# Five sets of seven products and one plain stretch in a SwiGLU layer, with three weight sums formed in device memory

## The reference

```python
x = x + merged @ w_o[layer]
h = rms_norm(x, ffn_norm_g[layer])
x = x + (jax.nn.silu(h @ w_ffn_gate[layer]) * (h @ w_ffn_up[layer])) @ w_ffn_down[layer]
return rms_norm(x, final_norm_g)
```

## Time and profile before

| | us |
|---|---|
| median of three runs | 377.54 (377.19 to 377.69) |
| the profiled execution | 377.2 |
| its span on the core | 375.4 |
| PE busy | 367.1 (98%) |
| DVE busy | 321.5 (86%) |
| ACT busy | 230.7 (61%) |
| POOL busy | 41.4 (11%) |
| data moved | 74.80 MB |
| granted TensorE clock | 0.995 of full speed |

### The profile page before, as it was taken

One profiled execution on the slowest core, in us unless ns is written; L12 is line 12 of the kernel. 1 busy time (PEld: TensorE's weight loads), 2 busy tenths in 40 slices (PEclk: granted clock), 3 DMA queues, 4 the chain that ended last, 5 costly groups with the idle time before them and its releaser, 6 DMA issues.

```text
span 375.4 us, 4744 instructions
## 1 busy us (share of the span) xinstructions
PE 367.1 (98%) x1847; PEld 309.0 (82%) x1847; DVE 321.5 (86%) x372; ACT 230.7 (61%) x267; POOL 41.4 (11%) x41
## 2 busy tenths in 40 slices
PE   7999999999999999999999999999999999999993
PEld 6998888788888888888888888888888888888882
DVE  4989987989867999989769669999999999999525
ACT  5767787676265956645447436955782892878205
POOL 2798020000000104000100000100100100000002
PEclk9999999999999999999999999999999999999998
DMA  8997255945270493899717902794796599360002
GB/s 284 282 296 266 60 182 207 320 143 210 57 281 0 66 345 120 321 353 308 281 55 276 358 39 55 179 384 172 184 359 236 129 308 347 113 248 33 0 2 112
DMA packets 41293, 74.80 MB, mean 199 GB/s; under 512 B 2316, under 2 KB 14648, under 8 KB 41272
## 3 DMA queue, kind: packets, MB, share of 16 engines
q1 hardware_dynamic: 38944, 70.03, 53.2%
q0 software_dynamic: 2112, 4.19, 6.6%
q10 hardware_dynamic: 216, 0.28, 0.2%
HBM read 73.46 MB, written 1.05 MB: 198 GB/s over the span
## 4 chain that ended last, share of the span: by engine, by line
PE 95%; DMA 1%; DVE 1%; issue 1%; POOL 0%; ACT 0%; POOLq 0%; SPq 0%; DVEq 0%; ACTq 0%
PE pp L1685 12%; PE pp L1687 12%; PE pp L1686 12%; PE pa L2069 7%; PE pa L2067 7%; PE pa L2068 7%; PE pp L1676 4%; PE pp L1665 3%; PE pp L1678 2%; PE pa L1676 2%; PE pa L2012 2%; PE pa L2010 2%; PE pa L1685 2%; PE pa L1687 2%; PE pa L2011 2%; PE pa L1686 2%
## 5 line engine op out<-in xcount | busy, mean ns | idle before, releaser
L1088 DVE TENSOR_TENSOR w_lo<-w_raw,w_hi 128x2048 fp32r<-128x2048 f32 x33 | 75.3, 2293 | 10.2 <-ACT w_hi L697 10.1
L970 ACT ACTIVATE w_hi<-w_raw 128x2048 fp32r<-128x2048 f32 x33 | 62.7, 1908 | 24.3 <-DVE w_raw L1536 24.3
L1556 DVE TENSOR_TENSOR w_lo<-w_raw,w_hi 128x2048 fp32r<-128x2048 f32 x33 | 74.6, 2283 | 0.2 <-ACT w_hi L970 0.2
L697 ACT ACTIVATE w_hi<-w_raw 128x2048 fp32r<-128x2048 f32 x33 | 62.6, 1912 | 19.6 <-DMA w_raw<-in_w_in 9.2
L1685 PE MATMUL pp<-w_hi,yT_hi 128*128 128x512 f32 (+1 forms) x104 | 40.5, 390 | 0.0
L1687 PE MATMUL pp<-w_lo,yT_hi 128*128 128x512 f32 (+1 forms) x104 | 40.3, 388 | 0.0
L1686 PE MATMUL pp<-w_hi,yT_lo 128*128 128x512 f32 (+1 forms) x104 | 40.3, 387 | 0.0
L1685 PE MATMUL pp<-w_hi,hT 128*128 128x512 f32 x96 | 38.0, 396 | 0.0
L1687 PE MATMUL pp<-w_lo,hT 128*128 128x512 f32 x96 | 37.4, 390 | 0.0
L1686 PE MATMUL pp<-w_hi,hT 128*128 128x512 f32 x96 | 37.4, 389 | 0.0
L2067 PE MATMUL pa<-w_hi,hT 128*128 128x512 f32 x64 | 24.9, 389 | 0.0
(11 more groups left out here) (341 smaller groups left out, 780.5 us busy)
## 6 DMA issues: line engine op xcount, KB each, us to landing
w_raw<-in_w_in SPq DMA_DIRECT2D x20, 1024.0 KB, 5.4
w_raw<-in_w_ffn_gate SPq DMA_DIRECT2D x11, 1024.0 KB, 8.9
w_raw<-in_w_ffn_up SPq DMA_DIRECT2D x11, 1024.0 KB, 8.5
w_raw<-in_w_ffn_down SPq DMA_DIRECT2D x11, 1024.0 KB, 7.9
w_raw<-in_w_o SPq DMA_DIRECT2D x4, 1024.0 KB, 5.3
x_sb<-in_w_ffn_gate POOLq DMA_DIRECT2D x3, 1024.0 KB, 9.3
w_raw<-in_w_out_attn SPq DMA_DIRECT2D x2, 1024.0 KB, 9.8
w_raw<-in_w_out_mlstm SPq DMA_DIRECT2D x2, 1024.0 KB, 5.2
```

The lines of the kernel that those rows point to most:

```text
L697: nc.scalar.activation(w_hi[:, slot_of(c), :], early_raw(c), ACT.Copy).then_inc(hi_ready, 1)
L970: nc.scalar.activation(w_hi[:, slot_of(c), :], form_raw(name, p), ACT.Copy).then_inc(hi_ready, 1)
L1088: nc.vector.tensor_tensor(w_lo[:, slot_of(c), :], early_raw(c), w_hi[:, slot_of(c), :].bitcast(F32), ALU.subtract).then_inc(lo_ready, 1)
L1556: nc.vector.tensor_tensor(w_lo[:, slot_of(c), :], form_raw(*FORM[c]), w_hi[:, slot_of(c), :].bitcast(F32), ALU.subtract).then_inc(lo_ready, 1)
```

## The change

Of the three plain stretches one stays and a fifth set takes the place of the two others: 256 plain columns and 2560 in sets. The first set now begins right behind the one plain stretch. Its sums `T1`, `T3` (here as `B22 + B12`) and `T2` are no longer made by DVE. Each is formed in a tensor `formed` in device memory, early in the kernel: SP copies one block there (`form_copy`), and POOL adds the other by an adding transfer (`form_grow`), written with the four rows of blocks `k` as the outermost index; the sums are then loaded like any chunk, `T2` straight into `x_sb`. POOL issues two of these adding transfers ahead of that of the mLSTM gate and the third right behind it. The splits run four chunks ahead of PE in place of five, and three during the first set. Some semaphores are merged to stay within their number, so that DVE's first use of the gate columns also waits for the biases.

```diff
-SETS = 4
-PLAIN = 3
+SETS = 5
+PLAIN = 1
+AHEAD_FORMED = {("T1", 0): ("B12", "B11"), ("T3", 0): ("B22", "B12"), ("T2", 0): ("B22", ("T1", 0))}
+STORED = {form: n for n, form in enumerate(AHEAD_FORMED)}
...
-    names = [("NG", 0), ("NU", 0), ("NG", 1), ("NU", 1), ("dN", 0), ("NG", 2), ("NU", 2)]
+    names = [("NG", 0), ("NU", 0)]
     for p in range(SETS):
-        before, after = (("dN", 1), ("dN", 2)) if p == 0 else (("dA", p - 1), ("dB", p - 1))
+        before, after = ([], [("dN", 0)]) if p == 0 else ([("dA", p - 1)], [("dB", p - 1)])
...
-C_SETS = C_FFN + 4
+C_SETS = C_FFN + 3
...
-    first = AT["B11", 0]
-    ahead = RING if c < first else LEAD
+    ahead = LEAD - 1 if c <= AT["B11", 0] else LEAD - 2 if c < AT["T4", 0] else LEAD - 1
     return min(max(c + ahead, split_to(c - 1)), C_FFN + len(AT) - 1)
...
+            def form_copy(name, p):
+
+                n, src = STORED[name, p], ffn_source(AHEAD_FORMED[name, p][0], p)
+                if n >= 2:
+                    sp.wait_ge(formed_copied[n % 2], 16 * (n // 2))
+                sp.dma_start(formed[n].rearrange("p (k n) -> p k n", k=4), src).then_inc(formed_copied[n % 2], 16)
...
+                if c == 8:
+                    form_copy("T1", 0)
+                    form_copy("T3", 0)
+                if c == 17:
+                    form_copy("T2", 0)
...
+                if (name, p) == ("B22", 0):
+
+                    src = ffn_source("T2", 0)
+                    sp.wait_ge(formed_grown, 16 * (STORED["T2", 0] + 1))
+                    sp.wait_ge(turned, 16)
+                    sp.dma_start(as_source(x_sb[:, :], src), src).then_inc(t2_loaded, 16)
...
+            def form_grow(name, p):
+
+                second, n = AHEAD_FORMED[name, p][1], STORED[name, p]
+                dst = formed[n].rearrange("p (k n) -> p k n", k=4)
+                src = ffn_source(second, p) if isinstance(second, str) else ffn_source(*second)
+                pool.wait_ge(formed_copied[n % 2], 16 * (n // 2 + 1))
+                if n:
+                    pool.wait_ge(formed_grown, 16 * n)
+                nc.gpsimd.dma_start(dst.rearrange("p k n -> k p n"), src.rearrange("p k n -> k p n"), accum_op=ALU.add
+                                    ).then_inc(formed_grown, 16)
+
+            form_grow("T1", 0)
             pool.wait_ge(w_exp_done, 2 * H_M)
...
+            form_grow("T3", 0)
             pool.wait_ge(lo_ready, GM["T2"] + 1)
             pool.wait_ge(gm_summed, 3)
             src = gm_source("B21")
             nc.gpsimd.dma_start(as_source(region_b[:, :], src), src, accum_op=ALU.add).then_inc(gm_grown, 16)
 
+            form_grow("T2", 0)
             pool.wait_ge(var_set, H_M)
...
-            dve.wait_ge(wif_loaded, 16)
+            dve.wait_ge(wif_loaded, 48)
...
             plain(0, 0)
             plain(0, 1)
-            plain(1, 0)
-            plain_turn(0)
-            plain(1, 1)
-            down("dN", 0)
-            plain_turn(1)
-            plain(2, 0)
-            plain(2, 1)
             for p in range(SETS):
```

More of the change, by code:

```diff
@@ L66, in places @@
 def places():
[L68 removed]
+    names = [("NG", 0), ("NU", 0)]
     for p in range(SETS):
[L70 to L72 removed]
+        before, after = ([], [("dN", 0)]) if p == 0 else ([("dA", p - 1)], [("dB", p - 1)])
+        names += [("B11", p), ("T1", p), ("T2", p), ("B22", p)] + before + [("T3", p)]
+        names += after + [("B21", p), ("T4", p)] if p + 1 < SETS else [("B21", p), ("T4", p)] + after
     names += [("dA", SETS - 1), ("dB", SETS - 1)]
@@ L77, with sum_count @@
 AT = places()
-C_SETS = C_FFN + 4
+C_SETS = C_FFN + 3
 def lo_place(name, p):
     return 2 * AT[name, p]
-def sum_count(name, p):
-    return 3 * p + SUMS.index(name) + 1
 def grown(name, p):
     return name == "T4" and p + 1 < SETS
+SUMMED = [(name, p) for p in range(SETS) for name in SUMS if not grown(name, p) and (name, p) not in STORED]
+def sum_count(name, p):
+    return SUMMED.index((name, p)) + 1
 def sums_ahead(name, p):
-    return {"T1": ("T1", "T2"), "T2": ("T3",), "B21": ("T4",) if p + 1 == SETS else ()}.get(name, ())
+    sums = {"T1": ("T1", "T2"), "T2": ("T3",), "B21": ("T4",)}.get(name, ())
+    return [part for part in sums if (part, p) in SUMMED]
 FORM = {c: form for form, c in AT.items()}
@@ L142, in landings @@
             place("B11", p, "T3")
-            place("B12", p, "T1")
+            place("T1" if ("T1", p) in STORED else "B12", p, "T1")
             place("B22", p, "B22")
-        elif name not in SUMS + ("B22",):
+        elif (name, p) == ("T1", 0):
+            place("T1", p, "T1")
+            place("B22", p, "B22")
+        elif name not in SUMS + ("B22",) or (name, p) == ("T3", 0):
             place(name, p, name)
@@ L193, in build @@
     down_k = w_ffn_down[0].rearrange("(k p) n -> p k n", p=P)
+    formed = nc.dram_tensor("formed", (len(STORED), P, CH), F32, kind="Internal").ap()
     with ExitStack() as ctx:
@@ L333, in form_raw @@
                 return x_sb[:, :]
-            return raw_of(LANDED[{"T1": "B12", "T3": "B11"}.get(name, name), p][0])
+            if name in SUMS and (name, p) not in STORED:
+                name = {"T1": "B12", "T3": "B11"}[name]
+            return raw_of(LANDED[name, p][0])
         def plain_banks(n):
@@ L479, in build @@
         w_grown = sem("w_grown")
+        t2_loaded = sem("t2_loaded")
+        formed_copied = [sem(f"formed_copied{n}") for n in range(2)]
+        formed_grown = sem("formed_grown")
         part_kept = sem("part_kept")
@@ L914, in _ @@
             act.wait_ge(gs_summed, 4)
-            nc.scalar.activation(third[0], s_d.rearrange("p (k n) -> p k n", k=4), ACT.Copy).then_inc(gm_third_hi, 1)
+            nc.scalar.activation(third[0], s_d.rearrange("p (k n) -> p k n", k=4), ACT.Copy).then_inc(third_hi_set, 1)
             split_hi(GM["B21"])
```

141 lines of the change are left out of this document (62 added, 79 removed).

## The result

The changed kernel takes 409.5 to 412.4 us where the kernel before takes 377.62 (median): a ratio of 1.0881, 95% interval 1.0837 to 1.0924. It is 33 us slower than before, and outside the range of 375.2 to 386 us.

What follows compares the result with a forecast made beforehand. PE was taken as the bound, with DVE having only 0.7 us in hand per set. -2.73 + 2.4 + 0.3 + 0.4 = +0.4 us on 377.2 gave 377.6 us, as median 377.9; range 375.2 to 386 us.

Steps and rivals of the forecast that it cites:

- The two earlier ones I cost at nothing: First two adding transfers, ahead of the gate's: no cost, as chunks already split cover loads late by some 5 us.
- as the nearest row is a transfer of the same size and kind: Third adding transfer, behind the gate's: reason for taking PE's wait at w_out_attn as 0.4 us, near the lower end.
- The rival: Adding transfers run on four DMA engines: PE waits 6 us near 72 us; 387 us, up to 397; chance 0.15.
- near a quarter: Sign of adding on four engines: software queue active for 20 us and more with a share near a quarter.
- at least 3 us: With adding on four engines, the third transfer would hold four loads behind the gate by at least this much more.
- The products saved: On PE, a fifth set replacing two plain stretches: 12 products fewer, 2.73 us less; 0.09 us more for transposition left out.
- The join of the first two sets: Between first and second set, DVE's chain takes 25.1 us against PE's 22.7: PE waits 2.4 us ahead of B11 and T2.
- the upper bound that the prediction named: At the first two sets' join: a wait of 3.5 us if the first set's T4 transfer lands a microsecond late.
- The third transfer at `w_out_attn`: Third adding transfer delays the second load of w_out_attn: PE waits 0.4 us, between 0 and 4.4.
- The two later places: First set's dA and third set's B11 come within 0.2 us of PE: 0.3 us for both, between 0 and 1.

Runs made afterwards that it cites:

- e4: The kernel before with the change's three copies and three adding transfers at the same places, read by nothing, semaphores merged; 409.23 us, ratio 1.0833.
- e5: As e4, but the adding transfers have the 128 partition rows as slowest dimension; 379.80 us, ratio 1.0061.
- e6: The kernel before with the first copy and first adding transfer alone, slowest dimension 4, read by nothing; 390.03 us, ratio 1.0331.
- e7: As e6, but the transfer has 8 entries in its slowest dimension; 378.45 us, ratio 1.0033.
- e2: The changed kernel with its three adding transfers written with the 128 partition rows as slowest dimension; 381.84 us, ratio 1.0106.
- e11: As e3, with the second set's first sum T1 also left out of the computation; 377.78 us, ratio 0.9996.
- e1: The changed kernel run once more with no edit; 410.14 us, ratio 1.0880.
- e3: The changed kernel without the three copies and adding transfers, the first set's T1, T3 and T2 sums left out; 379.79 us, ratio 1.0063.
- e8: As e2, with the third adding transfer issued behind POOL's lnv and lnr; 385.14 us, ratio 1.0210.

## Why the prediction was wrong

**The step that failed** is "The two earlier ones I cost at nothing", and with it "as the nearest row is a transfer of the same size and kind" for the third. Both took the gate's transfer as the model. It is the same in size, in kind and in the price of a packet (176 ns), but it goes over sixteen engines and the new ones over four. Those two steps were worth 0.4 us in the sum and measured 31.6 (e4), all but 2.4 of it by the loop order (e5).

**The rival was told and was given too little.** Its signs were all there: the software queue active for 35 us at 17.5% of 16 engines (it had said near a quarter, which is what both queues have together at 61 to 62 us), loads every 8.17 us (the rival had 8), PE idle near 72 us. The Trainium skill's rule (DMA: Bandwidth & Descriptors, "Why a DMA increments its semaphore by 16 and not by 1") made this rival the forecast. The traces of e6, e7 and e2 agree with it: 35.2, 18.3 and 10.4 us for slowest dimensions of 4, 8 and 128. I gave it 0.15 because no row of before had a transfer of that form. That was the error of judgement: what no row shows isn't thereby unlikely, and nothing in the profile spoke against it but a hope that loads slip between.

**The rival's size was off too**, 387 to 397 us for 410. Four terms were missing. At 72 us it had 6 us; the wait was 9.1. The rival ended at the late chunk's split. That was done at 78.9 us, 6 us after PE ran out of products, as reckoned; but on DVE's queue stood 2.6 us of other work between it and `yT_lo`, which PE waited for (the rows of DVE up to 81.49 us). The second transfer had no term; its wait was 4.6 us. The third had "at least 3 us" and made waits of 1.1, 3.2 and 3.6 us. And the slower products behind the waits, 7.3 us, were in no sum of mine.

**The products saved** (-2.73 us, with 0.09 for the transposition left out) came as reckoned. 1847 operations of PE became 1835. From its first product of the feed-forward layer (198.38 us) to the first set's `T3` (250.96 us) the kernel before needs 52.58 us, e11 18.98 (199.55 to 218.53): 33.60 us less, for a fifth set of 30.84, so 2.76 us are saved. e11's last product still starts 0.95 us later than before (369.77 against 368.82 us). Its projections start 1.18 us later (61.59 against 60.41 us), since DVE waits 1.26 us for a load of the first weights at 9.08 us, ahead of all that was changed; the wait ahead of `T2` is 1.77, and pauses too short for the list, at the second and third set, are some 0.76: 1.18 + 1.77 + 0.76 - 2.76 = 0.95. The late start is that execution's own (378.79 us, where e11's median is 377.78).

**The join of the first two sets** was right in place and mechanism, and 0.8 us short in size. PE waits 1.92 us ahead of `B11` (released by ACT's activation, as said) and 1.25 ahead of `T2` (released by the split): 3.2 us for 2.4. These are the rows of the trace of e1, PE, then ACT and DVE:

```profile
264.19 0.50 PE L2097 MATMUL pa<-w_hi,hT 128*128 128x512 f32 x1 [1.92 <-ACT region_a L1078]
...
272.05 0.47 PE L2097 MATMUL pa<-w_hi,hS 128*128 128x512 f32 x1 [1.25 <-DVE w_lo L1586]
```

```profile
253.06 1.92 ACT L997 ACTIVATE w_hi<-x_sb 128x2048 fp32r<-128x2048 f32 x1 [1.10 <-DMA x_sb<-in_w_ffn_gate]
```

```profile
255.01 2.29 DVE L1586 TENSOR_TENSOR w_lo<-x_sb,w_hi 128x2048 fp32r<-128x2048 f32 x1 [0.90 <-ACT w_hi L997]
```

The 0.90 us is the upper bound that the prediction named, the adding transfer for `T4` landing a little late. 2.4 + 0.9 is 3.3, and e2 has 3.3 (2.09 and 1.25). What the sum lacked is the clock: behind e3's wait it cost 1.5 us, and a wait ahead of `T2` doesn't show there. In e1's and e2's traces it cost nothing at this place.

**The third transfer at `w_out_attn`**, with all engines on it, is the term of 0.4 us. Its wait measured 1.09 us in e2 and 0.75 in e5, within its bounds of 0 and 4.4; the loads landed after 14.7 us ("more than 12").

**The two later places** had 0.3 us together. No wait shows there in e1's or e2's list; behind the join PE's rows fall back by another 0.18 us in e2.

With the transfers spread over the engines, the sum was 0.4 us and e2's last product starts 3.2 us later than before (371.99 against 368.82 us). Laid beside each other, the two traces give the terms: 0.5 us of a later start of the projections (60.89 against 60.41), 1.4 from there to the first product of the feed-forward layer, 1.09 of it the wait at `w_out_attn` (0.4 in the sum), 3.34 of waits at the join (2.4) and some 0.7 of short pauses around and behind it (0.3), less the 2.76. So even without the four engines the saving would have been given back: e2 is 1% slower. Why its runs spread from 380.42 to 383.62 us stays open. The mean clock doesn't say: it was 0.998 in the first and 0.996 in the last.

## What to carry to other kernels

Before a DMA is costed by a neighbour's duration, compare their access patterns: read off the slowest dimension of each side and ask over how many engines it can be split. A transfer on four engines isn't only longer (35 us for 10); it holds back every load that crosses those four engines, while the others idle (in e1's window of 60.6 to 64 us both queues moved 0.25 MB in 3.4 us; a load alone moved 0.41 MB in one). And where PE is the bound, count a wait with the slower products behind it, and look on the waiting engine's queue for what stands between the late item and the one that PE wants.

## What the hardware showed beside this

- A software-queue transfer of 512 rows of 2 KB counts 528 packets when it is spread over 16 engines, 1536 tiny ones more on four engines (e6) and 512 more where the slowest dimension is 8 (e7).
- An adding transfer from memory to memory, spread over all engines, lands after 9.3 and 10.4 us for 1 MB in e2, like one into SBUF (9.3 us there, 10.3 before); behind another on the queue it takes 16.4. Its packets hold an engine for 178 ns (345 of them are 113.1% of 16 engines in 3.4 us), where those of the gate's take 176 beside a load.
- After a wait of PE of 9.1 us the granted clock was 0.70 in the following 6 us, after one of 4.6 us it was 0.50 for 5.5 us, and after e3's of 2.4 us 0.62 for 4 us. After e2's waits of 1.1 and 2.1 us the trace shows no run of slower products, nor behind two waits of 2.0 and 1.4 us in a row in e8.
